# Decode attention in 2048-key steps: keys turned by VectorE in 32x32 blocks, scores in 32x64 tiles of the array

## The chip, the cores and the metric

One core of one Trainium2 chip runs the whole program in one launch. The metric is the device time in microseconds (us). The kernel before took 1918.83 us, the median of 3 runs (1914.7 to 1919.68).

## The reference, cut to what matters

The program is one inference step of a two-layer decoder: layer 0 is multi-head latent attention (MLA), layer 1 a recurrent block. It runs for a prompt of 1024 tokens and for 8 decode sequences of 8 new tokens each. Each decode sequence has 8192 past tokens, kept in pages of 128 tokens: 256 numbers of compressed latent (`ckv`) and 64 of rotated key (`kpe`) per token, all fp32. The change is in what the 8 sequences do with these pages:

```python
DEC_BATCH, DEC_SEQ, PAST_LEN, PAGE_SIZE = 8, 8, 8192, 128
N_HEADS, KV_LORA, QK_ROPE = 8, 256, 64
def attend_sample(q_lat, q_pe, ckv_past, kpe_past, ckv_new, kpe_new):
    s_past = mla_scores(q_lat, q_pe, ckv_past, kpe_past)   # q_lat.ckv + q_pe.kpe, scaled
    s_new = jnp.where(causal, mla_scores(q_lat, q_pe, ckv_new, kpe_new), NEG_INF)
    p = jax.nn.softmax(jnp.concatenate([s_past, s_new], axis=-1), axis=-1)
    return p_past @ ckv_past + p_new @ ckv_new             # the latents are keys and values
def mla_out(o_lat, z, w_uv, w_o):
    v = einsum('bthc,chv->bthv', o_lat, w_uv)
    return (v * silu(z)) @ w_o
# ckv_past = cache_ckv[page_table], kpe_past = cache_kpe[page_table]: pages in random order
```

With 8 heads and 8 tokens a sequence has 64 query rows, so two sequences (a pair) fill the 128 partitions of a score tile.

## The kernel before, in words

The program is a row of parts with a barrier between them: modulation, the input projection of layer 0, the latents, prompt attention, decode attention, the output projection of layer 0 (`out0`), and then the parts of layer 1. Inside a part each engine has its own instruction list, written in program order, and semaphores tie the lists together. So the order on an engine is the order in which the code is written.

`decode_attention` runs a hardware loop over 4 pairs of sequences. For each pair there is a step for the new tokens and 16 steps of 512 keys (`CHUNKS`). GpSimd loads raw pages by indirect DMA (`load`, L983), four chunks at a time into one of two slots. A token then lies on a partition, while a score matmul needs features on partitions. So TensorE turns the keys (`keys`, L1164): five PSUM banks per chunk, four transposes of 128x128 against the identity in each. Two of the banks belong to each sequence's `ckv`; the fifth holds the `kpe` of both, which GpSimd has put side by side before (L1003). ScalarE and VectorE copy these banks into `kT` (`keep_keys`, L1040: three on ScalarE, two on VectorE).

`scores` is then one matmul of 128x128 by 512 for `kpe` (L1179) and four of 128x64 by 512 for `ckv` (`both`, L1142), two for each sequence. `both` puts the two sequences into the left and right half of the array's columns. VectorE finds the row maximum (`maximum`, L1092 to L1096), ScalarE computes the exponential (L1061) and the factor that corrects earlier steps (L1059). TensorE turns the probabilities (`turn`, L1195), VectorE copies them out of PSUM (`keep_probs`, L1104), TensorE multiplies them by the raw pages (`values`, L1142, again through `both`), and VectorE adds the result to the running output (`accumulate`, L1114 and L1117). TensorE's order for chunk x is: `keys(x, 1..4)`, `turn(x)`, `keys(x+1, 0)`, `scores(x+1)`, `values(x)`. After the last pair a product with `w_uv` (L1232) and a multiplication by the gate (L1134) end the part.

`out0` multiplies the gated rows by `w_o`: SP loads the weights in eight pieces into three buffers (L1282), ScalarE and VectorE split each piece into a high and a low part, and TensorE runs three products for each piece. The gated prompt rows stay in the SBUF tensor `u_T` from prompt attention on.

Of the kernel before, what the change touches and what calls it, by code (L numbers as in the profile page):

```python
# [22 lines left out]
ds = bass.ds  # L23
# [475 lines left out]
def latents(nc, bank, io, k, u_T, a, outs):  # L499
# [3 lines left out]
    with ExitStack() as ctx:  # L503
# [17 lines left out]
        with nc.Block() as block:  # L521
# [18 lines left out]
            def _(act):  # L540
# [7 lines left out]
                act.activation(a["kpe_s"][:], kpe[:, NP:T], ACT.Copy).then_inc(kpe_hi, 1)  # L548
                for t in range(NT):
                    n, b = (P if t < 8 else NS), t % 2  # L550
                    act.wait_ge(rows_turned, t + 1)
                    if t >= 2:
                        act.wait_ge(rows_stored[b], 32 * (t // 2))
                    act.activation(rows_out[0:n, b, :], bank[0:n, t % 4, 0:KVL + ROPE], ACT.Copy).then_inc(rows_kept, 1)

            @block.vector
            def _(dve):
# [8 lines left out]
                dve.tensor_scalar(a["parts"][:].rearrange("p (b g s) -> p b s g", s=2, g=GROUPS),  # L566
                                  bank[:, 7, 0:NB * GROUPS].rearrange("p (b s g) -> p b s g", s=2, g=GROUPS),
                                  float(PPP), k["part_of_page"][:], ALU.mult, ALU.add).then_inc(pages_d, 1)
# [29 lines left out]
            def _(pe):  # L598
# [4 lines left out]
                pe.wait_ge(pages_d, 3)  # L603
# [26 lines left out]
def prompt_attention(nc, bank, io, k, u_T, a):  # L630
# [8 lines left out]
    with ExitStack() as ctx:  # L639
# [17 lines left out]
        unit, a_ev, d_ev, qpe_zero = sem("unit"), sem("a_ev"), sem("d_ev"), sem("qpe_zero")  # L657
        s_done, rowmax, m_done, e_done, r_done, pn_done = (sem(n) for n in ("s_done", "rowmax", "m_done", "e_done", "r_done", "pn_done"))
        pt_ps, pt_hi_d, pt_lo_d, pv_done, o_out = (sem(n) for n in ("pt_ps", "pt_hi_d", "pt_lo_d", "pv_done", "o_out"))
        A_N, D_N = 12, 16  # L660
# [5 lines left out]
        with nc.Block() as block:  # L666
            @block.sync
            def _(sp):
# [10 lines left out]
                load(0)  # L679
                with sp.Fori(1, NPAIR) as pr:  # L680
                    sp.wait_ge(unit, pr * U)
                    load(pr)

# [49 lines left out]
            def _(dve):  # L733
                dve.memset(a["qpe"][:], 0.0).then_inc(qpe_zero, 1)
                dve.wait_ge(qpe_zero, 1)
                with dve.Fori(0, NPAIR) as pr:
# [16 lines left out]
                    for h in range(2):  # L753
                        for q in range(2):

                            dve.tensor_copy(a["qpe"][ROPE * q:ROPE * q + ROPE, :, ds(pr * 2 * NTOK + (ROPE * q + NTOK * h), NTOK)],
                                            pe_rot[ROPE * h:ROPE * h + ROPE, NP:T].rearrange("p (c q t) -> p c q t", q=2, t=NTOK)[:, :, q, :]
                                            ).then_inc(d_ev, 1)
# [41 lines left out]
                    for h in range(2):  # L800
                        dve.tensor_copy(a["qlat"][:, :, :, ds(pr * 2 * NTOK + NTOK * h, NTOK)],
# [13 lines left out]
            def _(pe):  # L815
                with pe.Fori(0, NPAIR) as pr:
# [35 lines left out]
                    pe.wait_ge(d_ev, pr * D_N + 12)  # L852
                    project(1, lambda c: w_uk[:, c, P:2 * P], kv, VC, 256)
                    pe.wait_ge(d_ev, pr * D_N + 13)
# [51 lines left out]
                    pe.wait_ge(d_ev, pr * D_N + 16)  # L906
# [13 lines left out]
def decode_attention(nc, bank, io, k, u_T, a, outs):  # L920
# [7 lines left out]
    NPAIR, CHUNKS, SLOTS = NB // 2, PAGES // 4, 2  # L928
    STEPS, BLOCKS = CHUNKS + 1, 5
    S_BANK, PT_BANK, O_BANK, T_BANK = 0, 2, 3, 4  # L930
    HALF = H * NTOK
    with ExitStack() as ctx:
        sb = lambda n, shape, dt=F32: ctx.enter_context(nc.sbuf_tensor(n, shape, dt))
        sem = k["semaphore"]
        ckv = sb("ckv_pages", [P, SLOTS, 2, PAGE // PPP, KVL])
        kpe_raw = sb("kpe_pages", [P, SLOTS, 2, PAGE // PPP, ROPE])
        zero = sb("zero", [P, 2])
        kT = sb("k_T", [P, 2, BLOCKS, 512])

        free = u_T[:, 0:QC, :].rearrange("p c t -> p (c t)")  # L940
        prob = free[:, 0:1024].rearrange("p (b n) -> p b n", b=2)
        probT = free[:, 1024:2048].rearrange("p (b n) -> p b n", b=2)
        w_uv = free[:, 2048:4096].rearrange("p (c n) -> p c n", c=VC)
        kpe_r = u_T[:, N_M, 0:1024].rearrange("p (b j s e) -> p b j s e", b=2, j=4, s=2)
        o_T = u_T[:, KPE_M, 0:1024].rearrange("p (c b q) -> p c b q", c=VC, b=NB)
        parts_next = sb("parts_next", [P, 8], I32)
        tick = sb("tick", [1, 1])
        ticked, parts_set, kpe_pair_set = sem("ticked"), sem("parts_set"), sem("kpe_pair_set")
        s_new = sb("s_new", [P, NTOK])
# [866 lines left out]
```

## Time and profile before

| what | value |
|---|---|
| time, median of 3 runs | 1918.83 us (1914.7 to 1919.68) |
| span of the profiled execution | 1918.3 us |
| TensorE matmul busy, whole span | 1617.1 us (84%) |
| VectorE, ScalarE, GpSimd busy, whole span | 796.3, 627.4, 223.0 us |
| prompt attention | 347.0 to 776.4 us |
| decode attention | 776.4 to 1324.6 us |
| `out0` | 1324.6 to 1451.0 us |

The span is the time on the chip from the first to the last instruction of the profiled execution; it lies 0.5 us under the median. PE is TensorE's matmul side and PEld its weight loads, DVE is VectorE, ACT ScalarE, POOL GpSimd and SP the engine that issues most DMAs. A busy share over the whole span mixes parts with different limits, so the readings below are of the decode part. The stretch between two parts is found where all engines wait for the barrier. A record of an fp32 matmul stands for one of its two passes, so eight records are four matmuls.

### The profile page before, as it was taken

How to read it: one execution, taken by the hardware profiler on the slowest of the kernel's cores; microseconds unless marked ns; L12 is line 12 of the kernel's file. 1: busy time of each engine (PE TensorE's matmuls, PEld its weight loads, DVE VectorE, ACT ScalarE, POOL GpSimd, SP SyncE). 2: the span in 40 equal slices, each digit the busy share in tenths (PEclk: the TensorE clock that was granted, in tenths of full speed). 3: DMA queues.
4: the chain of work that ended last, by engine and by line, in shares of the span. 5: the costliest groups of instructions: out<-in, count | busy, mean ns of one | idle time of the engine just before them, and what ended most of it. 6: DMA issues, size and time to landing. Idle time of an engine off the chain costs nothing. (4 is left out here: it accounts for less than half of the span.)

```text
span 1918.3 us, 26899 instructions
## 1 busy us (share of the span) xinstructions
PE 1617.1 (84%) x10091; PEld 1274.6 (66%) x10091; DVE 796.3 (42%) x1403; ACT 627.4 (33%) x1022; POOL 223.0 (12%) x219
## 2 busy tenths in 40 slices
PE   4779996688889798599898998998996999870497
PEld 1379995577777677466555565655875999870285
DVE  1240003364645537255444454544226541239633
ACT  3231212142333324233333332333433232355232
POOL 0000000000000000222222222220121000006121
PEclk7779997799989899699999999998998999995699
DMA  9821100110100000525253245222322111100322
GB/s 333 299 56 45 44 22 24 57 28 1 27 0 27 0 0 0 243 110 220 111 201 143 115 201 217 113 110 80 118 72 64 44 44 33 44 1 0 123 88 77
DMA packets 80578, 169.42 MB, mean 88 GB/s; under 512 B 9941, under 2 KB 51803, under 8 KB 76410
## 3 DMA queue, kind: packets, MB, share of 16 engines
q1 hardware_dynamic: 71290, 84.49, 13.4%
q0 software_dynamic: 9216, 83.89, 10.9%
q8 instruction: 55, 0.90, 0.2%
q14 instruction: 17, 0.14, 0.0%
HBM read 157.91 MB, written 10.45 MB: 88 GB/s over the span
## 5 line engine op out<-in xcount | busy, mean ns | idle before, releaser
L80 PE MATMUL bank<-in_x_hi,in_w_hi 128*128 128x272 f32 x992 | 289.8, 292 | 19.9 <-DVE in_x_lo L413 19.8
L82 PE MATMUL bank<-in_x_hi,in_w_lo 128*128 128x272 f32 x992 | 288.8, 291 | 0.0
L81 PE MATMUL bank<-in_x_lo,in_w_hi 128*128 128x272 f32 x992 | 287.4, 290 | 0.0
L80 PEld LDWEIGHTS bank<-in_x_hi,in_w_hi 128*128 128x128 f32 x992 | 188.6, 190 | 20.5 <-issue 19.8
L81 PEld LDWEIGHTS bank<-in_x_lo,in_w_hi 128*128 128x128 f32 x992 | 188.9, 190 | 0.0
L82 PEld LDWEIGHTS bank<-in_x_hi,in_w_lo 128*128 128x128 f32 x992 | 188.4, 190 | 0.0
L1164 PE MATMUL bank<-c_ident,ckv_pages 128*128 128x128 f32 x1024 | 143.0, 286 | 12.4 <-DMA ckv_pages<-in_cache_ckv,page_parts 12.4
L1040 ACT ACTIVATE k_T<-bank 128x512 f32<-128x512 f32 x192 | 114.3, 598 | 109.8 <-PE bank L1164 109.8
L1164 PEld LDWEIGHTS bank<-c_ident,ckv_pages 128*128 128x128 f32 x1024 | 119.5, 147 | 35.8 <-issue 23.1
L403 DVE TENSOR_TENSOR in_w_lo<-in_w_raw,in_w_hi 128x1024 fp32r<-128x1024 f32 x31 | 37.9, 1224 | 239.2 <-ACT in_w_hi L355 239.1
L1142 PE MATMUL bank<-k_T,q_pair 128*64 128x512 f32 x512 | 124.5, 607 | 0.0
L1142 PE MATMUL bank<-ckv_pages,u_T 128*64 128x256 f32 x1024 | 121.6, 379 | 3.1 <-DVE u_T L1104 3.1
L80 PE MATMUL bank<-out_w_hi,out_g_hi 128*128 128x512 f32 (+1 forms) x288 | 114.8, 398 | 6.5 <-DVE out_w_lo L1391 6.5
L1092 DVE TENSOR_REDUCE d_stat<-bank 128x1 f32<-128x512 f32 x64 | 44.3, 691 | 178.0 <-PE bank L1142 178.0
L1142 PEld LDWEIGHTS bank<-ckv_pages,u_T 128*64 128x64 f32 x1024 | 73.4, 137 | 65.8 <-issue 34.2
L81 PE MATMUL bank<-out_w_lo,out_g_hi 128*128 128x512 f32 (+1 forms) x288 | 113.6, 394 | 0.0
L82 PE MATMUL bank<-out_w_hi,out_g_lo 128*128 128x512 f32 (+1 forms) x288 | 113.5, 394 | 0.0
L355 ACT ACTIVATE in_w_hi<-in_w_raw 128x1024 fp32r<-128x1024 f32 x31 | 32.8, 1059 | 240.2 <-PE bank L82 203.5
L1040 DVE COPY k_T<-bank 128x512 f32<-128x512 f32 x128 | 88.3, 691 | 37.1 <-PE bank L1164 31.7
L1003 POOL TENSOR_TENSOR u_T<-kpe_pages,zero 128x512 f32<-128x512 f32 x64 | 66.3, 1045 | 254.2 <-PE bank L1164 170.9
L823 PE MATMUL bank<-u_T,w_q 128*128 128x272 f32 x384 | 92.3, 401 | 3.1 <-DVE q_lo L739 3.1
L1059 ACT ACTIVATE d_stat<-d_stat 128x1 f32<-128x1 f32 x64 | 18.8, 295 | 228.6 <-DVE d_stat L1096 228.6
(272 smaller groups left out, 2950.4 us busy)
## 6 DMA issues: line engine op xcount, KB each, us to landing
u_T<-in_w_ada SPq DMA_DIRECT2D x12, 2048.0 KB, 14.3
in_w_raw<-in_r_w_in SPq DMA_DIRECT2D x16, 512.0 KB, 3.9
in_w_raw<-in_a_w_in SPq DMA_DIRECT2D x15, 512.0 KB, 4.0
x_tiles<-in_x_prompt SPq DMA_DIRECT2D x8, 512.0 KB, 9.3
out_w_raw<-in_a_w_o SPq DMA_DIRECT2D x8, 512.0 KB, 3.6
out_x_in<-in_x_prompt SPq DMA_DIRECT2D x8, 512.0 KB, 4.0
x_mid<-out_x_new SPq DMA_DIRECT2D x8, 512.0 KB, 2.9
u_T<-in_r_w_o SPq DMA_DIRECT2D x8, 512.0 KB, 8.4
```

The costliest lines, as they stand in the source:

```text
L80: pe.matmul(out, w_hi, x_hi, start=start, stop=False)
L81: pe.matmul(out, w_hi, x_lo, start=False, stop=False)
L82: return pe.matmul(out, w_lo, x_hi, start=False, stop=stop)
L355: act.activation(w_hi[:, b, :, :], w_raw[:, b, :, :], ACT.Copy).then_inc(w_hi_done, 1)
L403: dve.tensor_tensor(w_lo[:, b, :, :], w_raw[:, b, :, :], w_hi[:, b, :, :].bitcast(F32), ALU.subtract).then_inc(w_lo_done, 1)
L823: mm = pe.matmul(r[:, q, 0:cols], weights(c), x[:, c, cols * q:cols * q + cols], start=(c == 0), stop=(c == nch - 1))
L1003: pool.tensor_tensor(kpe_r[:, c % 2, :, :, :].rearrange("p j s e -> p s j e"), kpe_raw[:, c // 4 % SLOTS, :, 4 * (c % 4):4 * (c % 4) + 4, ...
L1040: ins = eng.activation(dst, src, ACT.Copy) if eng is nc.scalar else eng.tensor_copy(dst, src)
L1059: act.activation(col(CORR, x), col(M, x - 1), ACT.Exp, scale=SCALE, bias=col(NM, x)).then_inc(corr_d, 1)
L1092: dve.tensor_reduce(col(RM), bank[:, S_BANK + x % 2, :], AX.X, ALU.max).then_inc(rmax_d, 1)
L1142: mm = pe.matmul(out[HALF * s:HALF * s + HALF, :], w(s), x(s), start=start, stop=stop, tile_position=(0, HALF * s))
L1164: mm = pe.transpose(bank[:, T_BANK + n % 4, P * j:P * j + P], src, k["ident"][:])
```

## The change

Decode attention is written anew. A step now has 2048 keys of a pair of sequences, 16 steps in all, 4 for a pair, unrolled. What takes the place of what:

- Pages: GpSimd issues four indirect loads of 1 MB a step into 12 units (three steps' worth) and two of 0.5 MB for `kpe` into one buffer each.
- Keys: VectorE transposes 32x32 blocks straight from the raw pages in SBUF (`keys_T`), 10 blocks of 32 features for two sequences, 20 instructions of 128x512 a step, into a ring of 7 blocks. TensorE no longer turns keys, nothing is copied out of PSUM for them, and GpSimd's reordering of `kpe` goes.
- Since each 32-partition strip then holds other keys, the queries are copied into all four strips (`qrep`, 24 small DMAs for a pair, issued by SP). A score matmul is 32 rows by 64 columns by 512 keys; eight of them (4 strips x 2 sequences) belong to a block, and each strip writes a PSUM bank of its own (banks 0 to 3).
- The maximum and the exponential take 128x2048 in one instruction. The probabilities are turned in four groups of four, each copied out of PSUM by ScalarE.
- The new tokens' scores and values are added to the first step of a pair.
- The gated prompt rows are stored to DRAM pair by pair in prompt attention (the last store is waited for there). `out0` loads them back tile by tile on SP's queue, ahead of the weights for the first two tiles, and has six weight buffers instead of three. Two small copies (`z_s`, `k_new`) and two more index computations go into the latents.

Core of the diff (removed lines that the section on the kernel before tells of are left out):

```diff
-    NPAIR, CHUNKS, SLOTS = NB // 2, PAGES // 4, 2
-    STEPS, BLOCKS = CHUNKS + 1, 5
+    NPAIR, STEPS, PER = NB // 2, NB // 2 * GROUPS, GROUPS
+    KEYS, J, BLK, RING, UNITS = GP * PAGE // 4, PAGE // PPP, 10, 7, 12
...
+                def queries(pr):
+                    for q in range(4):
+                        rows = slice(SQ * q, SQ * q + SQ)
+                        for bb in range(4):
+                            sp.dma_start(qrep[rows, pr % 2, :, 2 * bb:2 * bb + 2, :].rearrange("p s v q -> p s (v q)"),
+                                         a["qlat"][SQ * bb:SQ * bb + SQ, 2 * pr:2 * pr + 2, :, :].rearrange("p s v q -> p s (v q)")
...
+                queries(0)
                 sp.dma_start(ckv_new[:], outs[4][0].rearrange("b t c -> t b c")).then_inc(new_in, 16)
+                queries(1)
                 sp.dma_start(w_uv, io["a_w_uv"][0].rearrange("(k p) h n -> p k (h n)", p=P)).then_inc(wuv_in, 16)
+                for pr in range(2, NPAIR):
+                    sp.wait_ge(s_blk, BLK * PER * (pr - 1))
+                    queries(pr)
...
+                def keys_T(n, blocks):
+                    for b in blocks:
+                        at = BLK * n + b
+                        if at >= RING:
+                            dve.wait_ge(s_blk, at - RING + 1)
+                        for s in range(2):
...
+                            dve.transpose(kT[:, at % RING, s, :].rearrange("p (j c) -> p j c", c=SQ), src).then_inc(t_done, 1)
...
+                keys_T(0, range(BLK))
+                for n in range(STEPS):
+                    maximum(n)
+                    if n + 1 < STEPS:
+                        keys_T(n + 1, range(4))
+                    if n:
+                        accumulate(n - 1)
+                    if n + 1 < STEPS:
+                        keys_T(n + 1, range(4, BLK))
...
+                def scores(n):
...
+                    for b in range(BLK):
+                        at = BLK * n + b
+                        pe.wait_ge(t_done, 2 * at + 2)
+                        for q in range(4):
+                            rows = slice(SQ * q, SQ * q + SQ)
+                            for s in range(2):
+                                mm = pe.matmul(bank[HALF * s:HALF * s + HALF, q, :], qrep[rows, pr % 2, s, b, :], kT[rows, at % RING, s, :],
+                                               start=b == 0, stop=b == BLK - 1, tile_position=(SQ * q, HALF * s))
+                        mm.then_inc(s_blk, 1)
...
+                scores(0)
+                for n in range(STEPS):
+                    turn(n)
+                    if n + 1 < STEPS:
+                        scores(n + 1)
+                    if n % PER == 0 and n:
+                        finish(n // PER - 1)
+                    values(n)
...
+                    sp.wait_ge(o_out, pr * 8)
+                    store(pr - 1)
+                sp.wait_ge(o_out, NPAIR * 8)
+                store(NPAIR - 1)
+                sp.wait_ge(g_out, 16 * NPAIR)
...
-        NRAW = KC if final else 3
+        NRAW = KC if final else 6
...
+                for t in range(0 if final else 2):
+                    sp.dma_start(g_raw[:, t, :, :], g_T[0].rearrange("c p t -> p c t")[:, :, t * P:t * P + P]).then_inc(g_ld[t], 16)
```

How TensorE's list changes. First one 512-key chunk of the kernel before, as written; four of these make 2048 keys (the names behind "waits" are of semaphores that several parts share; x2 or x7 behind a row counts equal rows that follow):

```order
L1164 MATMUL bank<-c_ident,ckv_pages 128x128 [waits part_out]
L1164 MATMUL bank<-c_ident,ckv_pages 128x128 x3
L1164 MATMUL bank<-c_ident,u_T 128x128 [waits x_in1]
L1164 MATMUL bank<-c_ident,u_T 128x128 x3
L1195 MATMUL bank<-c_ident,u_T 128x128 [waits ident_in,x_turned]
L1195 MATMUL bank<-c_ident,u_T 128x128 x3
L1179 MATMUL bank<-k_T,qpe_pair 128x512 [waits x_turned,sq_done]
L1142 MATMUL bank<-k_T,q_pair 64x512 x4
L1142 MATMUL bank<-ckv_pages,u_T 64x256 [waits d_o_done,ident_in]
L1142 MATMUL bank<-ckv_pages,u_T 64x256 x7
```

Then TensorE in one 2048-key step of the changed kernel: turning the probabilities of step n (L1169), the scores of step n+1 (L1159, here two of the ten blocks), the values of step n (L1189, here the first two of four groups):

```order
L1169 MATMUL bank<-c_ident,u_T 128x128 [waits d_pt_sb,gate_b_in]
L1169 MATMUL bank<-c_ident,u_T 128x128 x3
L1169 MATMUL bank<-c_ident,u_T 128x128 [waits d_pt_sb]
L1169 MATMUL bank<-c_ident,u_T 128x128 x3
L1159 MATMUL bank<-u_T 64x512 [waits xn_done,gate_b_in]
L1159 MATMUL bank<-u_T 64x512 x7
L1159 MATMUL bank<-u_T 64x512 [waits xn_done]
L1159 MATMUL bank<-u_T 64x512 x7
L1189 MATMUL bank<-ckv_pages,u_T 64x256 [waits d_pt_sb,d_o_done]
L1189 MATMUL bank<-ckv_pages,u_T 64x256 x7
L1189 MATMUL bank<-ckv_pages,u_T 64x256 [waits d_pt_sb]
L1189 MATMUL bank<-ckv_pages,u_T 64x256 x7
```

The twenty key transposes and the `kpe` matmul of each chunk are gone from TensorE; each block of eight score matmuls now waits for VectorE's transposes (`t_done`, shown as xn_done).

VectorE in a chunk of the kernel before, with the two key copies (L1040), the probabilities' copy, the maximum and the accumulation:

```order
L1040 COPY k_T<-bank 128x512 [waits ms_done,part_done]
L1040 COPY k_T<-bank 128x512 [waits part_done]
L1104 COPY u_T<-bank 128x512 [waits gate_b_in,x_out]
L1092 TENSOR_REDUCE d_stat<-bank 128x1 [waits ms_done]
L1094 TENSOR_TENSOR d_stat<-d_stat 128x1 [waits rstd_done]
L1096 TENSOR_SCALAR d_stat<-d_stat 128x1 [waits modt_done]
L1114 SCALAR_TENSOR_TENSOR d_stat<-d_stat 128x1 [waits mod_kept,x_turned]
L1117 SCALAR_TENSOR_TENSOR o_acc<-o_acc,d_stat,bank 128x256 [waits d_o_done,gate_b_in]
```

VectorE in a step of the changed kernel: the maximum of step n over 2048 keys (L1083 to L1087), then the transposes of step n+1, of which the first eight stand before the accumulation of step n-1 and twelve behind it (the last two pairs of these are of `kpe`):

```order
L1083 TENSOR_REDUCE d_stat<-bank 128x1 [waits x_turned]
L1084 TENSOR_TENSOR d_stat<-d_stat 128x1 [waits d_own]
L1087 TENSOR_SCALAR d_stat<-d_stat 128x1 [waits d_own]
L1071 STREAM_TRANSPOSE u_T<-ckv_pages 128x512 [waits w_ada_in3,w_ada_in2,x_turned]
L1071 STREAM_TRANSPOSE u_T<-ckv_pages 128x512 [waits x_in1,x_in0]
L1071 STREAM_TRANSPOSE u_T<-ckv_pages 128x512 [waits x_turned]
L1071 STREAM_TRANSPOSE u_T<-ckv_pages 128x512
L1098 TENSOR_TENSOR d_stat<-d_stat 128x1 [waits modt_done,gate_b_in]
L1100 COPY o_acc<-bank 128x256 [waits d_pv_h]
L1071 STREAM_TRANSPOSE u_T<-kpe_pages 128x512 [waits part_done,x_turned]
L1071 STREAM_TRANSPOSE u_T<-kpe_pages 128x512 [waits part_out]
```

VectorE's three copies a chunk give way to 20 transposes a step; x_turned is here `s_blk`, the count of scored blocks, which frees a place in the ring of seven.

## Rows read from the trace of the kernel before

**Rows 1.** Windows: stretch, us, busy us PE PEld DVE ACT POOL, clock, DMA, GB/s.
```profile
776.40:1324.60 548.20, 504.32 (x3300) 309.96 (x3300) 247.32 (x557) 181.13 (x408) 131.09 (x151) 0.95 0.39 156
784.00:788.00 4.00, 0.00 (x0) 0.00 (x0) 0.00 (x0) 0.00 (x0) 2.64 (x3) 0.50 1.02 426
56.30:59.40 3.10, 3.09 (x17) 0.60 (x16) 0.00 (x0) 2.17 (x3) 0.00 (x0) 0.61 1.05 388
```
**Rows 2.** Waits in the decode part: total us, times, longest us.
```profile
ACT d_stat L1059 <- DVE d_stat L1096: 228.6, 64, 5.0
DVE d_stat L1092 <- PE bank L1142: 178.0, 64, 4.8
PE bank L1164 <- DMA ckv_pages<-in_cache_ckv,page_parts: 12.4, 1, 12.4
```
**Rows 3.** Timeline of TensorE over one 512-key chunk: start us, us, instructions.
```profile
808.35 1.90 PE L1142 MATMUL bank<-ckv_pages,u_T 128*64 128x256 f32 x16
810.18 1.53 PE L1164 MATMUL bank<-c_ident,ckv_pages 128*128 128x128 f32 x12
811.55 0.60 PE L1164 MATMUL bank<-c_ident,u_T 128*128 128x128 f32 x4
811.98 0.60 PE L1195 MATMUL bank<-c_ident,u_T 128*128 128x128 f32 x4
812.42 0.60 PE L1164 MATMUL bank<-c_ident,ckv_pages 128*128 128x128 f32 x4
813.02 1.10 PE L1179 MATMUL bank<-k_T,qpe_pair 128*128 128x512 f32 x2
814.04 1.94 PE L1142 MATMUL bank<-k_T,q_pair 128*64 128x512 f32 x8
815.81 1.90 PE L1142 MATMUL bank<-ckv_pages,u_T 128*64 128x256 f32 x16
```
**Rows 4.** Timeline of TensorE in the modulation: eight matmuls in 32-column tiles.
```profile
56.30 3.09 PE L253 MATMUL bank<-u_T,c_T 128*32 128x512 f32 x16
```
**Rows 5.** Groups of VectorE by line and shape: busy us, mean ns, idle before.
```profile
L1092 DVE TENSOR_REDUCE d_stat<-bank 128x1 f32<-128x512 f32 x64 | 44.3, 691 | 178.0 <-PE bank L1142 178.0
L769 DVE TENSOR_REDUCE att_stat<-bank 128x1 f32<-128x1024 f32 x8 | 9.8, 1224 | 1.1
L779 DVE TENSOR_SCALAR prob<-prob,att_stat 128x512 f32<-128x512 f32 x8 | 3.9, 486 | 0.3
L1639 DVE TENSOR_TENSOR_SCAN lru_r<-lru_a,u_T 128x1024 f32<-128x1024 f32 x8 | 24.4, 3044 | 0.0
L1094 DVE TENSOR_TENSOR d_stat<-d_stat 128x1 f32<-128x1 f32 x64 | 10.6, 166 | 2.2
L1117 DVE SCALAR_TENSOR_TENSOR o_acc<-o_acc,d_stat,bank 128x256 f32<-128x256 f32 x64 | 30.7, 480 | 37.8 <-PE bank L1142 37.8
```
**Rows 6.** Groups of ScalarE by line and shape.
```profile
L711 ACT ACTIVATE prob<-bank,att_stat 128x1024 f32<-128x1024 f32 x8 | 8.9, 1114 | 0.0
L711 ACT ACTIVATE prob<-bank,att_stat 128x128 f32<-128x128 f32 x8 | 3.0, 370 | 6.7 <-DVE att_stat L772 6.7
L1040 ACT ACTIVATE k_T<-bank 128x512 f32<-128x512 f32 x192 | 114.3, 598 | 109.8 <-PE bank L1164 109.8
```
**Rows 7.** Timeline at the start of the decode part.
```profile
777.26 1.12 POOL L983 DMA_INDIRECT ckv_pages<-in_cache_ckv,page_parts  x1 [0.72 <-POOL zero L975]
793.79 3.68 PE L1164 MATMUL bank<-c_ident,ckv_pages 128*128 128x128 f32 x16 [12.38 <-DMA ckv_pages<-in_cache_ckv,page_parts]
```
**Rows 8.** Timeline at its end: last values, then the product with w_uv.
```profile
1312.95 1.95 PE L1142 MATMUL bank<-ckv_pages,u_T 128*64 128x256 f32 x16 [0.78 <-DVE u_T L1104]
1317.05 5.99 PE L1232 MATMUL bank<-u_T 128*128 128x64 f32 x32 [0.67 <-ACT u_T L1072]
```
**Rows 9.** DMA issues: KB each, us from issue to landing.
```profile
x_mid<-out_x_new SPq DMA_DIRECT2D x8, 512.0 KB, 2.9
```
**Rows 10.** Costliest groups: the first product of an output projection.
```profile
L80 PE MATMUL bank<-out_w_hi,out_g_hi 128*128 128x512 f32 (+1 forms) x288 | 114.8, 398 | 6.5 <-DVE out_w_lo L1391 6.5
```
**Rows 11.** Costliest groups: weight loads of the values product.
```profile
L1142 PEld LDWEIGHTS bank<-ckv_pages,u_T 128*64 128x64 f32 x1024 | 73.4, 137 | 65.8 <-issue 34.2
```

More of the change, by code:

```diff
@@ new lines, in _ @@
+                own = Chain(dve, own_d)
+                def keys_T(n, blocks):
[4 more added lines that the diff above has]
+                        for s in range(2):
+                            if b == 0:
+                                for half in range(2):
+                                    dve.wait_ge(ckv_in[unit(n, s, half)], 16 * (n // 3 + 1))
+                            if b == 8:
+                                dve.wait_ge(kpe_in[s], 16 * (n + 1))
+                            if b < 8:
+                                u, c0 = unit(n, s, 0), P * (b % 2) + SQ * (b // 2)
+                                src = ckv[:, u:u + 2, :, c0:c0 + SQ].rearrange("p u j c -> p (u j) c")
+                            else:
+                                src = kpe[:, s, :, SQ * (b - 8):SQ * (b - 8) + SQ]
+                            dve.transpose(kT[:, at % RING, s, :].rearrange("p (j c) -> p j c", c=SQ), src).then_inc(t_done, 1)
@@ new lines, in new_scores @@
+                        seq, out = 2 * pr + s, bank[HALF * s:HALF * s + HALF, X_BANK, 0:NTOK]
+                        new = slice(NTOK * seq, NTOK * seq + NTOK)
+                        pe.matmul(out, a["qpe"][:, seq, :], a["kpe_s"][0:ROPE, new], start=True, stop=False, tile_position=(0, HALF * s))
+                        for v in range(VC):
+                            mm = pe.matmul(out, a["qlat"][:, seq, v, :], a["k_new"][:, v, new], start=False, stop=v == VC - 1,
+                                           tile_position=(0, HALF * s))
@@ new lines, in values @@
+                def values(n):
+                    pr, g = divmod(n, PER)
+                    if n:
+                        pe.wait_ge(o_done, n)
+                    halves = [slice(HALF * s, HALF * s + HALF) for s in range(2)]
+                    if g == 0:
+                        pe.wait_ge(ptn_sb, pr + 1)
+                        for s in range(2):
+                            pe.matmul(bank[halves[s], O_BANK, 0:KVL], p_new_T[:, halves[s]], ckv_new[:, 2 * pr + s, :], start=True, stop=False,
+                                      tile_position=(0, HALF * s))
+                    for j in range(J):
+                        if j % 4 == 0:
+                            pe.wait_ge(pt_sb, 4 * n + j // 4 + 1)
+                        for s in range(2):
+                            mm = pe.matmul(bank[halves[s], O_BANK, 0:KVL], probT[:, P * j + HALF * s:P * j + HALF * s + HALF],
+                                           ckv[:, unit(n, s, j // 8), j % 8, :], start=g > 0 and j == 0, stop=j == J - 1,
+                                           tile_position=(0, HALF * s))
+                        if j % 8 == 7:
+                            mm.then_inc(pv_h, 1)
@@ L1228, in _ @@
+                finish(NPAIR - 1)
                 pe.wait_ge(wuv_in, 16)
@@ L1705, in build, with rows_of @@
         x_mid = nc.dram_tensor("x_mid", [T, D], F32).ap()
+        gated = nc.dram_tensor("gated", [KC, P, NP], F32).ap()
+        def rows_of(prompt, decode):
+            return lambda t: decode if isinstance(t, int) and t == NT - 1 else prompt[ds(t * P, P), :]
         with ExitStack() as mla:
```

478 lines of the change are left out of this document (202 added, 276 removed).

## The prediction, made before the changed kernel ran

> **What bounds the kernel now.** I read the windows first: decode takes 548.2 us, and TensorE has matmuls in flight for 504.3 of them, while VectorE is busy 247.3 and ScalarE 181.1 [rows 1]. The waits say the same from the other side: VectorE's maximum waits 178.0 us for TensorE's scores, ScalarE 228.6 us for VectorE, but TensorE itself has only one large wait, 12.4 us for the first pages [rows 2]. So TensorE's own list is the length of this part. One chunk of that list, from one `values` to the next, takes 815.81 - 808.35 = 7.46 us [rows 3]; 64 of them make 477 of the 548. DMA isn't near the bound: the part moves 156 GB/s on average and 426 in a loaded stretch [rows 1]. A 2048-key step needs 5.24 MB, which is 12.3 us at that rate.
>
> **Where a chunk goes.** From start to start of the groups [rows 3]: `values` 1.83, sixteen `ckv` transposes and four of `kpe` 1.37 + 0.43 + 0.60 = 2.40, turning the probabilities 0.44, the `kpe` matmul 1.02, the four `ckv` score matmuls 1.77. Four chunks are 29.84 us.
>
> **TensorE's new step.** The transposes of keys and the `kpe` matmul go. `values` is unchanged: 4 x 1.83 = 7.32. Turning needs 16 transposes, 4 x 0.44 = 1.76; but the third group waits for ScalarE's first copy out of PSUM and the fourth for the second, at 0.60 each [rows 6], so I take 2.5. The scores are the doubtful term. Ten blocks of eight matmuls of 32 rows by 64 columns replace the rest. In the trace two matmuls that lie side by side in the columns cost as much as one: four of them in 1.77 us is 0.88 a pair, no more than the full-width `kpe` matmul's 1.02 [rows 3]. And eight matmuls in 32-column tiles took 3.09 us at a granted clock of 0.61 [rows 1, 4]; one after another at even full speed they would take 8 x 0.88 = 7.0. So column tiles run at once, four of them too. Tiles that differ in rows are not in the trace. If the four strips also run at once, a block is one pair's time, 0.88, and I take 0.90 for the starts of eight tiles; if the strips queue behind one another it is 4 x 0.88 = 3.5. I take 0.90: the nearest row, the four column tiles, shows the array running as many tiles as it is cut into. Scores are then 9.0, and with 0.3 for the changes of tile shape a step is 9.0 + 2.5 + 7.3 + 0.3 = 19.1 us in place of 29.84.
>
> The Trainium skill, "TensorE: Matmul & The Clock Gate", Part 3 (Measured speedup vs the span model), lists four row tiles of 32 rows with 512 columns at 3.07 times the speed of one, not 4. By that page a block would be 0.88 x 4 / 3.07 = 1.15, an estimate, and the time about 1756 us. No run before shows four row tiles.
>
> **VectorE's new step.** Its new work is 20 transposes of 128x512 from SBUF to SBUF. No row shows one. The cheapest row of that size is 0.486 (a multiplication by a scalar, SBUF to SBUF); the dearest per element is the scan, 3.044 for 1024, so 1.52 for 512 [rows 5]. The nearest rows are plain reads of 512 elements, at 0.69. I take 0.70: 14.0 us. The maximum over 2048 continues 0.691 at 512 and 1.224 at 1024 by 1024 x 1.04 ns to 2.29. Three small instructions at about 0.17 (as L1094) and the accumulation's 0.48 add 1.0, so 17.3 us of work. After the last transpose VectorE waits until that block is scored, some 1.3, before the next maximum: 18.6. That is just under TensorE's 19.1, so the two engines nearly tie, and each 0.01 us on a transpose above about 0.725 adds 0.2 to every step.
>
> **ScalarE's chain.** Between the last block of step n+1 and turning it stand the maximum chain, 2.3 + 0.35, and the exponential over 2048. That one continues 0.370 at 128 and 1.114 at 1024, 0.83 ns for an element, to 1.96 [rows 6]; with the read of its sum some 2.2. Together 5.0, and `values(n)` at 7.3 lies beside it. If that cover went, it would be 5.0 a step. GpSimd's reordering disappears, but nothing waited for it on the path.
>
> **The decode part, from its start.** The first pages came 793.79 - 776.40 = 17.4 us into the part before, after two `ckv` loads and two of `kpe` [rows 7]; the first three of the new loads, each half as large, let VectorE begin, and I take +15. SP has 24 small copies of queries to issue first, before the new tokens' latents; I take them as covered by these 15 us. Twenty transposes, 14.0, and the last block: the first scores end at +30. The maximum and twenty transposes more: the second end at +47.7. Fourteen steps at 19.1 are 267.4, so +315.1. Then values 7.3, turn 2.5, values 7.3 and the tail. From the end of the last `values` (1312.95 + 1.95) to the end of the part it took 9.7 before [rows 1, 8], and that work is unchanged: +341.9. Three further pair starts at about 1.3 (new tokens' scores, two transposes of the output) make 346. That is 202 us less than 548.2.
>
> **The rest.** The stores of gated rows overlap the next pair, but the last is waited for: 2.9 for 512 KB [rows 9] and 1.2 for as much again at 426 GB/s, +4.1. Two copies of 128x512 in the latents: 2 x 0.60 [rows 6] = +1.2. In `out0` the six weight buffers can take back at most the 6.5 us that both output projections wait for split weights [rows 10], and two 512 KB tiles ahead of the weights delay the first by 2.5 at 426 GB/s, up to 5 with their short runs. I take -2, with -6.5 and +5 as ends. Prompt attention loses two small VectorE copies a pair, which I count as nothing, since VectorE waits there. Sum: -202 + 4.1 + 1.2 - 2 = -199. From the span of 1918.3 that gives 1719.6, and with the 0.5 by which the median lies over the span, 1720 us.
>
> **Rivals.**
> 1. *The strips queue.* Nothing in the trace excludes it. A block is then 3.5 and a step 35 + 10.1 = 45; the first scores end at +50, the second 7.5 + 35 later, fourteen steps add 631 and the end 31: about 755 against 548, so near 2128 us, slower. With a block at b the part is about 195 + 160b, which passes 548 at b = 2.2: from there the kernel is slower. 6 in 100.
> 2. *The strips overlap in part.* If two of the sixteen weight loads of a block, 0.137 each [rows 11], aren't hidden, it is 0.90 + 0.27 = 1.17; 2.7 more a step, 15 times, less what VectorE's near tie takes up anyway, is some 38: 1758 us. That loads of weights run under matmuls in flight (the part has 310.0 us of them and still 504.3 of matmuls in 548.2 [rows 1]) speaks against it, the number of small instructions in a block for it. The page of the skill named above lands near the same time by its own figure. 14 in 100.
> 3. *VectorE becomes the bound.* At t for a transpose its step is 20t + 4.6. With 0.85 it is 21.6, 2.5 more than 19.1, and with the dearer first two steps some 42: 1762 us. With 1.0 it is 24.6, 1810 us. At the scan's 1.52 it is 35, and the whole comes to about 1980, slower; the turn lies near 1.35. 17 in 100, of which 2 beyond the turn. The Trainium skill, "VectorE: DVE Perf Modes" (The three transpose paths), gives 311 ns for a 128x128 transpose of 2-byte numbers; four of them would be 1.24, an estimate, and the time about 1885. "Vector Engine (DVE) Microarchitecture Reference", § 3.8, says instead that the transpose sustains one element per cycle and lane, by which it is no dearer than a copy. The plain reads at 0.69 are what the rows have.
> 4. *The queries come late.* If the 24 small copies land behind the 12 MB of pages, which take 30 us at 426 GB/s, the first scores end at +40 instead of +30: 1730 us. 10 in 100.
>
> **How the numbers follow.** The forecast has 53 in 100, with its own range 1698 to 1740: down to 1698 if transposes cost 0.6, blocks 0.86 and turning 2.0, up to 1740 with a step of 19.8 and the dear end of `out0`. Rivals 2 and 4 and the cheap half of 3 lie below 1800, so the range is 1692 to 1800, which leaves out rival 1, the dear half of rival 3, and little below. A difference under 0.3%, 5.8 us, can't be told from none. Slower: rival 1 and the end of rival 3, 0.08; the same, 0.02 at the turn between them; faster, 0.90.
>
> **What would show it.** A score block (L1159) of 0.9 us from the first of its eight matmuls to the next block's first; transposes (L1071) of 0.7; TensorE busy for nearly all of the decode part and VectorE over 85% of it, with short waits on either side; a step of about 19 us from one maximum to the next. The forecast is wrong if blocks take 2 us or more, if VectorE is busy throughout while TensorE waits for `t_done`, or if the decode part is far from 346 us while blocks and transposes cost what I say.

## The result, and the profile after

| | before | after |
|---|---|---|
| time, median | 1918.34 us (1914.7 to 1919.68, 4 runs) | 1727.55 us (1725.26 to 1729.77, 4 runs) |
| ratio | 1 | 0.9002, 95% interval 0.8986 to 0.9017 |
| span of the profiled execution | 1918.3 us | 1728.0 us |
| latents, from first to last instruction (as in the rows below) | 47.0 us | 47.7 us |
| prompt attention | 427.8 us | 429.5 us |
| decode attention | 547.6 us | 350.3 us |
| `out0` | 125.9 us | 125.6 us |

The kernel is 10% faster; 1720 us was forecast. The modulation, in which nothing changed, took 102.5 us in the profile of before and 107.2 in that of after. Over all kernels profiled here it varies between 102.5 and 107.2, so 4.7 us of the comparison of spans is not owed to the change.

Two windows of the changed kernel, with the columns of [rows 1]: the decode part (351 us here, with the barrier at its end) and its steady middle. The clock is the granted clock of TensorE as a share of 2.4 GHz: 0.50 is the 1.2 GHz level.

```profile
783.30:1134.30 351.00, 304.98 (x3948) 165.99 (x3949) 244.93 (x417) 73.24 (x124) 90.07 (x96) 0.94 0.71 251
857.00:1100.00 243.00, 239.25 (x3170) 128.92 (x3169) 195.91 (x335) 58.14 (x99) 69.31 (x75) 1.00 0.78 282
```

In that middle VectorE's maximum still waits for TensorE's scores (columns of [rows 2]):

```profile
DVE d_stat L1083 <- PE bank L1159: 44.1, 13, 3.8
```

In the middle TensorE is busy 239 of 243 us at the full clock. It is still the bound; VectorE is busy 81%. About 46 us of the part's 351 are without a matmul, most of them at the start.

One step in that middle, TensorE's timeline; [rows 3] is the answering piece of before:

```profile
999.71 5.57 PE L1189 MATMUL bank<-ckv_pages,u_T 128*64 128x256 f32 x50
1005.21 1.09 PE L1169 MATMUL bank<-c_ident,u_T 128*128 128x128 f32 x8
1006.61 1.14 PE L1169 MATMUL bank<-c_ident,u_T 128*128 128x128 f32 x8 [0.31 <-ACT u_T L1042]
1007.69 8.84 PE L1159 MATMUL bank<-u_T 32*64 32x512 f32 x160
1016.46 7.13 PE L1189 MATMUL bank<-ckv_pages,u_T 128*64 128x256 f32 x64
1023.51 1.09 PE L1169 MATMUL bank<-c_ident,u_T 128*128 128x128 f32 x8
```

Turning takes 1007.69 - 1005.21 = 2.48 us, the ten blocks of scores 1016.46 - 1007.69 = 8.77, so 0.877 a block, and the values 1023.51 - 1016.46 = 7.05. The 0.31 is the wait for ScalarE's copies out of PSUM.

The groups that answer to [rows 5, 6]:

```profile
L1071 DVE STREAM_TRANSPOSE u_T<-ckv_pages 128x512 f32<-128x512 f32 x256 | 155.6, 675 | 33.8 <-DMA ckv_pages<-in_cache_ckv,page_parts 20.5
L1159 PE MATMUL bank<-u_T 32*64 32x512 f32 x2560 | 144.4, 600 | 0.0
L1028 ACT ACTIVATE u_T<-bank,d_stat 128x2048 f32<-128x2048 f32 x16 | 31.5, 1968 | 201.1 <-DVE d_stat L1087 201.1
```

The record of a transpose lasts 0.675 us on average; back to back the records overlap, and 256 of them keep VectorE busy for 155.6 us, 0.61 each. The end of the part, to be read beside [rows 8]:

```profile
1119.66 7.13 PE L1189 MATMUL bank<-ckv_pages,u_T 128*64 128x256 f32 x64
1128.83 3.76 PE L1218 MATMUL bank<-u_T 128*128 128x64 f32 x32 [0.56 <-ACT u_T L1047]
```

And the largest wait that TensorE has in the decode part, with the columns of [rows 2]:

```profile
PE bank L1137 <- DMA ckv_new<-out: 38.6, 1, 38.6
```

It began 5.5 us before the part, so 33.1 of it lie in the part, where the pages' 12.4 us stood before: the first scores wait for the new tokens' latents, 64 KB. The start in the timeline of VectorE, SP and TensorE:

```profile
796.83 0.71 DVE L1071 STREAM_TRANSPOSE u_T<-ckv_pages 128x512 f32<-128x512 f32 x1 [18.48 <-DMA ckv_pages<-in_cache_ckv,page_parts]
799.15 0.49 SPq L987 DMA_DIRECT2D ckv_new<-out  x1
799.61 7.83 DVE L1071 STREAM_TRANSPOSE u_T<-ckv_pages 128x512 f32<-128x512 f32 x13 [2.06 <-DMA ckv_pages<-in_cache_ckv,page_parts]
816.41 0.38 PE L1137 MATMUL bank<-kpe_new,qpe_T 64*64 64x8 f32 x2 [38.63 <-DMA ckv_new<-out]
818.07 11.80 PE L1159 MATMUL bank<-u_T 32*64 32x512 f32 x160
820.19 1.30 DVE L1071 STREAM_TRANSPOSE u_T<-ckv_pages 128x512 f32<-128x512 f32 x2 [12.76 <-PE bank L1159]
830.00 2.29 DVE L1083 TENSOR_REDUCE d_stat<-bank 128x1 f32<-128x2048 f32 x1 [4.84 <-PE bank L1159]
```

Below, +13 means 13 us after the start of the part.

The pages are there at 796.83, 13.5 us into the part, and VectorE fills its ring of seven blocks (14 transposes) by 807.4. Then it waits 12.76 us, because no block is scored. `ckv_new` is issued at 799.15, behind 24 copies of queries, and lands 17 us later. The first scores end at 829.9, 46.6 us into the part.

What shares the DMA engines with the copies is in the next rows: GpSimd's next loads of pages, and the packets of the pages (q0, from GpSimd) and of the copies (q1, from SP), with their MB and share of the 16 engines' time, first from 800 to 810, then from 812 to 816:

```profile
824.58 0.94 POOL L1010 DMA_INDIRECT kpe_pages<-in_cache_kpe,page_parts  x1 [28.17 <-DVE u_T L1071]
```

```profile
q0 software_dynamic: 571, 3.69, 96.1%
q1 hardware_dynamic: 571, 0.18, 8.1%
```

```profile
q1 hardware_dynamic: 1531, 0.57, 99.9%
q0 software_dynamic: 47, 0.25, 17.5%
```

GpSimd stands for 28.17 us before the third load of `kpe`, until VectorE has read the first. So ten loads are ahead of the copies, 9.4 MB and not the 12 of the fourth rival. While they stream, the two queues move the same number of packets, but a packet of pages has 6.5 KB on average and one of the copies 0.3 KB: the copies get 5% of the bytes. When the pages end, the copies' packets go nearly seven times as fast, 383 a us instead of 57. That is in line with copies that land only with the last pages; the second experiment tests it.

### The profile page after: what moved, and what is told of

Read it like the earlier page. It is cut to its first block and busy times, and to the rows that moved or that the text cites. A ratio compares the mean times of both kernels' runs of the same rounds, so it can differ in the third digit from the quotient of the medians.

```text
span 1728.0 us, 26291 instructions
## 1 busy us (share of the span) xinstructions
PE 1413.8 (82%) x10739; PEld 1128.7 (65%) x10739; DVE 793.1 (46%) x1256; ACT 520.4 (30%) x740; POOL 181.9 (11%) x164
## 3 DMA queue, kind: packets, MB, share of 16 engines
q1 hardware_dynamic: 88378, 95.50, 17.3%
## 5 line engine op out<-in xcount | busy, mean ns | idle before, releaser
L1071 DVE STREAM_TRANSPOSE u_T<-ckv_pages 128x512 f32<-128x512 f32 x256 | 155.6, 675 | 33.8 <-DMA ckv_pages<-in_cache_ckv,page_parts 20.5
L1159 PE MATMUL bank<-u_T 32*64 32x512 f32 x2560 | 144.4, 600 | 0.0
L1003 POOL DMA_INDIRECT ckv_pages<-in_cache_ckv,page_parts x64 | 60.1, 939 | 770.3 <-POOLq L1699 670.5
L1189 PE MATMUL bank<-ckv_pages,u_T 128*64 128x256 f32 x1024 | 114.0, 381 | 0.0
L1159 PEld LDWEIGHTS bank<-u_T 32*64 32x64 f32 x2560 | 55.6, 134 | 77.0 <-issue 61.9
L1189 PEld LDWEIGHTS bank<-ckv_pages,u_T 128*64 128x64 f32 x1024 | 72.1, 137 | 45.3 <-issue 10.6
L1028 ACT ACTIVATE u_T<-bank,d_stat 128x2048 f32<-128x2048 f32 x16 | 31.5, 1968 | 201.1 <-DVE d_stat L1087 201.1
L831 PEld LDWEIGHTS bank<-u_T,w_q 128*128 128x128 f32 x384 | 74.2, 195 | 19.9 <-DVE q_lo L750 4.8
L735 ACT ACTIVATE pt_hi<-bank 128x512 fp32r<-128x512 f32 (+2 forms) x96 | 43.8, 489 | 119.9 <-PE bank L889 119.9
L1321 POOL TENSOR_TENSOR out_x_new<-out_x_new,out_x_in 128x1024 f32<-128x1024 f32 (+1 forms) x18 | 43.0, 2386 | 245.9 <-DVE out_x_new L1408 245.9
```

The costliest lines, as they stand in the source:

```text
L735: act.activation(pt_hi[:, 4 * g:4 * g + n, slot:slot + P], bank[:, 4 + gi % 2, 0:P * n].rearrange("p (j q) -> p j q", q=P), ACT.Copy).then ...
L831: mm = pe.matmul(r[:, q, 0:cols], weights(c), x[:, c, cols * q:cols * q + cols], start=(c == 0), stop=(c == nch - 1))
L1003: pool.indirect_dma_start(ckv[:, u, :, :].rearrange("p j c -> p (j c)"), None, io["cache_ckv"][0].rearrange("n (q j) c -> (n q) (j c)", q= ...
L1071: dve.transpose(kT[:, at % RING, s, :].rearrange("p (j c) -> p j c", c=SQ), src).then_inc(t_done, 1)
L1159: mm = pe.matmul(bank[HALF * s:HALF * s + HALF, q, :], qrep[rows, pr % 2, s, b, :], kT[rows, at % RING, s, :], start=b == 0, stop=b == BLK ...
L1189: mm = pe.matmul(bank[halves[s], O_BANK, 0:KVL], probT[:, P * j + HALF * s:P * j + HALF * s + HALF], ckv[:, unit(n, s, j // 8), j % 8, :], ...
```

## The experiments

**Is it the latents alone that are late?** TensorE's wait for them is moved to where the values product needs them.

```diff
-                pe.wait_ge(new_in, 16)
                 scores(0)
...
+                        if pr == 0:
+                            pe.wait_ge(new_in, 16)
                         pe.wait_ge(ptn_sb, pr + 1)
```

> The changed kernel, but TensorE waits for the new tokens' latents (ckv_new) only where their values product needs them, not ahead of the first scores. In the changed kernel that wait was 38.6 us. Theory (all small copies of SP lie behind the 12 MB of pages): the 24 copies of queries land no earlier than ckv_new does, so TensorE now waits for them instead; the first scores start at most 3 us earlier and the time stays within 1723 to 1731 us. Rival (ckv_new alone is late, because it is issued 25th): the queries are there by about +22 us in the decode part, the first scores start some 9 us earlier, and the time is near 1718 us.

1729.14 us, one run. The wait only changed its name:

```profile
811.74 11.07 PE L1159 MATMUL bank<-u_T 32*64 32x512 f32 x160 [31.29 <-DMA u_T<-qpe_T]
```

Its decode part begins at 778.7, so the first scores start at +33, where they started at +34.8. The queries are as late as the latents; the theory stands, with ten loads in place of its 12 MB.

**Do the small copies wait behind the pages?** On top of that edit, GpSimd holds back the pages from step 1 on (those of step 2 were behind the 28 us of standing anyway), so 5.2 MB instead of 9.4 are ahead of the copies.

```diff
                 for n in range(STEPS):
+                    if n == 1:
+                        pool.wait_ge(qrep_in[0], 16 * 24)
+                        pool.wait_ge(new_in, 16)
```

> As the run before, and GpSimd issues the pages of steps 1 and 2 only when the queries of the first pair and ckv_new have landed. Theory (small copies wait behind the pages): only 5 MB of pages are ahead of them, they land near +22 us instead of +33, the first scores end near +32 instead of +46.5, and the pages of step 1 come in time or a few us late; the time falls by 8 to 14 us, to 1714 to 1720. Rival (the copies are slow by themselves, 24 at about 0.65 us of issue and their own latency): they land at +33 as before, and the pages of step 1 come late on top, so the time rises by 5 us or more.

1717.62 us, ratio to before 0.895 (0.8935 to 0.8965), an interval that lies under that of the changed kernel. Its decode part begins at 779.1:

```profile
802.27 10.74 PE L1162 MATMUL bank<-u_T 32*64 32x512 f32 x160 [21.45 <-DMA u_T<-qpe_T]
819.27 9.01 DVE L1074 STREAM_TRANSPOSE u_T<-ckv_pages 128x512 f32<-128x512 f32 x15 [2.32 <-DMA ckv_pages<-in_cache_ckv,page_parts]
```

The queries are complete at +23, ten us sooner than with ten loads ahead of them. Of these 23 us SP's issuing takes 15.8: it issues the 24 copies from 783.33 to 799.1 in the changed kernel, and as long here. The pages of step 1 come 2.3 us late, which was the price expected.

**What if the queries are copied in good time?** The copies of pairs 0 and 1 are moved into prompt attention, right after its last pair has produced the queries. The last store moves into the decode part, and the wait for the latents moves as in the first experiment (the last not in the diff).

```diff
-                sp.wait_ge(o_out, NPAIR * 8)
-                store(NPAIR - 1)
-                sp.wait_ge(g_out, 16 * NPAIR)
+                sp.wait_ge(g_out, 16 * (NPAIR - 1))
+                sp.wait_ge(d_ev, NPAIR * D_N)
+                for pr in range(2):
+                    copy_queries(sp, u_T, a, pr, q_out)
+                sp.wait_ge(q_out, 16 * 48)
...
-                queries(0)
                 sp.dma_start(ckv_new[:], outs[4][0].rearrange("b t c -> t b c")).then_inc(new_in, 16)
-                queries(1)
+                sp.dma_start(a["gated"].rearrange("c p t -> p c t")[:, KC - 2:KC, :], u_T[:, N_M - 2:N_M, 0:NP]).then_inc(st_out, 16)
+                sp.wait_ge(st_out, 16)
```

> The queries of pairs 0 and 1 are copied in prompt attention, as soon as its last pair has produced them (they have 100 us of cover there); the last store is issued in the decode part, behind ckv_new; and ckv_new is waited for only by the first values product. Theory (the late queries cost all of what the first scores lost, and nothing else is late there): the first scores follow VectorE's transposes and end about 30 us into the decode part instead of 46.5, decode takes some 335 us, prompt attention 4 us less, the time is 1704 to 1711. Rival (the next thing is late: the pages of steps 1 and 2 beside the 1 MB store, or TensorE at the low clock): the first two scores end later than +32 and +50, and the time is 1712 to 1720.

1710.84 us (1706.79 to 1720.07 over 5 runs), ratio to before 0.8924 (0.8902 to 0.8946). This is faster than the kernel before and the changed kernel. Its profile is of the fastest of the five runs and that of the changed kernel of the slowest of four, so the parts are compared and not the spans. The decode part takes 336.0 us, 14.3 less than in the changed kernel, and prompt attention 422.2:

```profile
792.99 11.79 PE L1165 MATMUL bank<-u_T 32*64 32x512 f32 x160 [17.94 <-DVE u_T L1076]
804.88 2.29 DVE L1088 TENSOR_REDUCE d_stat<-bank 128x1 f32<-128x2048 f32 x1 [1.03 <-PE bank L1165]
```

The part begins at 773.5. The two other edits by themselves left the decode part at 350.0 (the store, next run) and 352.0 (the latents' wait, first run), so the 14 us need the copies moved; what that brings with the latents' wait in its old place wasn't run. TensorE now waits for VectorE's transposes, and the first scores end at +31.3, where the prediction had put them (+30).

**The last store by itself.** As in the run just told, without moving the queries.

> The changed kernel, but the last store of gated rows (1 MB) is issued in the decode part, behind the queries, and is no longer waited for at the end of prompt attention. Theory (that wait is the 4.1 us of the prediction, and nothing in decode needs the store before its fifth step): prompt attention ends about 4 us earlier, the decode part stays at 349 to 352 us, the time is 1722 to 1725. Rival (the 1 MB only adds to the traffic in which the queries are already late): decode grows by as much, and the time stays within 1726 to 1731.

1723.9 us, ratio 0.8983 (0.8966 to 0.9001), an interval that overlaps that of the changed kernel, so the parts have to decide. Prompt attention took 422.0 us, decode 350.0. In the changed kernel the last instruction of VectorE in prompt attention ends at 778.34 and the next part begins at 783.3; before, these were 775.40 and 776.4 [rows 1]. The wait thus costs about 4, as the theory has it. The rest of the 7.5 us by which this profile's prompt attention is shorter isn't explained: in the other kernels, which keep the store's wait, it varied from 426.6 to 432.6, and the run with the queries in prompt attention, which has no such wait either, took 422.2.

**Do the strips run at once?** Strips 2 and 3 are left out after the first block.

```diff
-                        for q in range(4):
+                        for q in range(2 if b else 4):
```

> Leaves out half of the scores: strips 2 and 3 are scored in the first of the ten blocks only, so nine blocks have four matmuls instead of eight. Theory (the strips run at once, a block lasts as long as one pair of column tiles): a block stays at 0.88 us, the step at 18.3 us and the time at 1722 to 1730 us. Rival (the strips share the array's time): a block falls to about 0.45 us, the scores to about 5 us, and the step to VectorE's pace of about 16.7, so the time falls by 20 us or more, below 1708.

1737.04 us, one run: with half the matmuls the scores take as long as before, 871.77 - 863.02 = 8.75 us against 8.77:

```profile
818.08 17.34 PE L1159 MATMUL bank<-u_T 32*64 32x512 f32 x88
863.02 8.81 PE L1159 MATMUL bank<-u_T 32*64 32x512 f32 x88
871.77 7.13 PE L1189 MATMUL bank<-ckv_pages,u_T 128*64 128x256 f32 x64
```

So a block lasts as long with two strips as with four, and as long as one pair of column tiles (0.88 [rows 3]). The time missed the expected 1722 to 1730, and the first row says where: the first scores took 17.34 us instead of 11.80, at a low clock. Windows of this run from the first score matmul on and of the third scores:

```profile
818.00:824.00 6.00, 6.00 (x38) 1.87 (x41) 3.06 (x5) 0.00 (x0) 0.00 (x0) 0.50 0.45 122
824.00:830.00 6.00, 6.00 (x32) 1.72 (x28) 1.06 (x4) 0.00 (x0) 4.25 (x5) 0.50 0.73 254
830.00:836.00 6.00, 5.43 (x28) 1.23 (x20) 0.50 (x1) 0.00 (x0) 1.35 (x2) 0.50 0.99 391
863.00:871.70 8.70, 8.70 (x89) 2.97 (x88) 5.22 (x9) 0.73 (x2) 1.94 (x3) 1.00 0.98 382
```

And of the changed kernel:

```profile
818.00:824.00 6.00, 6.00 (x58) 2.01 (x65) 3.01 (x5) 0.00 (x0) 0.00 (x0) 0.50 0.44 110
824.00:830.00 6.00, 5.87 (x112) 1.87 (x96) 1.12 (x5) 0.00 (x0) 4.20 (x5) 0.99 0.81 261
```

With two strips the granted clock stays at 0.50, the 1.2 GHz level, all through the first scores; with four it was 0.99 from the seventh us on. In both runs TensorE had stood for 38 us before, but for 1.7 us of the new tokens' scores. The third scores ran at 1.00 with two strips too, so two strips don't hold the clock down once it is up.

**What would strips in turn cost?** Each strip's matmuls wait for those of the strip before.

```diff
                         for q in range(4):
+                            if q:
+                                pe.wait_ge(strip, 3 * at + q)
...
-                        mm.then_inc(s_blk, 1)
+                            mm.then_inc(strip if q < 3 else s_blk, 1)
```

> Each strip's two matmuls of a block wait until those of the strip before have ended, so the four strips run in turn; the result is the same. This prices the prediction's first rival. Theory (the strips' concurrency is worth 3 x 0.88 us a block, and a wait for one's own result costs something on top): a block takes 3.5 to 4.2 us, 160 of them add 420 to 530 us, the time is 2145 to 2260 us, slower than the kernel before. Rival (the strips shared more of the array's time than the trace shows, and running alone each is shorter): a block of 2.5 or less, under 1990 us.

2591.58 us, one run, far above what was expected. A stretch of scores and the windows say why:

```profile
899.38 46.37 PE L1162 MATMUL bank<-u_T 32*64 32x512 f32 x118
```

```profile
900.00:950.00 50.00, 48.11 (x136) 7.64 (x134) 3.22 (x5) 0.00 (x0) 1.87 (x2) 0.50 0.07 21
1500.00:1550.00 50.00, 48.23 (x190) 13.16 (x182) 11.47 (x19) 4.79 (x8) 3.75 (x4) 0.60 0.17 60
```

118 records are 7.4 blocks, so a block takes 6.3 us. The price was worked out at the full clock, 4 x 0.88, but TensorE ran at a granted clock of 0.50 to 0.60, though matmuls were in flight 48 of 50 us. At 0.50 a pair takes 1.73 (the 17.34 us above, for ten blocks), so four in turn would take 6.9: the low clock accounts for the excess over 3.5. So the run shows that strips held in turn by waits make the kernel slower than the one before, but not what they would cost at the full clock, and why the clock stays low isn't shown.

**How far is VectorE from being the bound?** Three runs: four transposes of a step done twice, eight done twice, and eight cut to 32 of 512 elements (the last not in the diff). Each was run once.

```diff
+                            if n and 4 <= b < 6:      # the second run: b < 8
+                                own.step(dve.transpose(kT[:, at % RING, s, :].rearrange("p (j c) -> p j c", c=SQ), src))
                             dve.transpose(kT[:, at % RING, s, :].rearrange("p (j c) -> p j c", c=SQ), src).then_inc(t_done, 1)
```

> Four transposes of a step (blocks 4 and 5) are done twice, 24 instead of 20; the result is the same. A transpose measured 0.605 us from start to start, and one that is waited for 0.67. Theory (VectorE's step is its work plus about 1.3 us of waiting for the last block, 20 x 0.605 + 4.6 = 16.7, beside TensorE's 18.3): it becomes 16.7 + 4 x 0.67 = 19.4, 1.1 over TensorE, so 15 steps add about 16 us: 1740 to 1748 us. Rival (all of the 3.2 to 3.7 us that VectorE waits at each maximum is free): 2.7 us fit in, and the time stays within 1723 to 1731.

> Eight transposes of a step are done twice, 28 in all; the result is the same. Theory (VectorE's step is 16.7 + 8 x 0.67 = 22.1, 3.8 above TensorE's): 15 steps add 57 us, the time is 1775 to 1792 us, and the rise over the run with four more (1745.5) is about 40. Rival (more of VectorE's waiting is free, and four more cost what they did for another reason): under 1765.

> From step 1 on, 8 of the 20 transposes of a step turn 32 of their 512 elements only, so their blocks are scored with stale keys; this takes about 4 us from VectorE's step of 16.7. Theory (TensorE's list is the bound, with VectorE 1.6 us a step behind it): the step stays at 18.3 us and the time at 1722 to 1731 us. Rival (the two engines nearly tie, as the prediction put it, and each waits for the other in turn): the step falls by 0.5 us or more and the time below 1720.

Four more: 1745.49 us, a step in the middle of a pair 964.13 - 944.74 = 19.39 from one maximum to the next (19.4 expected):

```profile
944.74 2.29 DVE L1085 TENSOR_REDUCE d_stat<-bank 128x1 f32<-128x2048 f32 x1 [1.28 <-PE bank L1161]
964.13 2.29 DVE L1085 TENSOR_REDUCE d_stat<-bank 128x1 f32<-128x2048 f32 x1 [1.27 <-PE bank L1161]
```

Eight more: 1794.17 us, slightly over the range; steps of 22.4 to 23.9 where 22.1 was expected, and 48.7 us over the run with four more where about 40 was. So the formula is 0.3 to 1.8 us a step short there. TensorE now waits twice in the scores for a block:

```profile
860.75 5.41 PE L1161 MATMUL bank<-u_T 32*64 32x512 f32 x96
866.93 1.12 PE L1161 MATMUL bank<-u_T 32*64 32x512 f32 x16 [0.77 <-DVE u_T L1073]
869.61 3.49 PE L1161 MATMUL bank<-u_T 32*64 32x512 f32 x48 [1.56 <-DVE u_T L1073]
```

Eight shorter: 1730.77 us, the step 883.62 - 865.31 = 18.31, as in the changed kernel:

```profile
865.31 2.29 DVE L1084 TENSOR_REDUCE d_stat<-bank 128x1 f32<-128x2048 f32 x1 [4.38 <-PE bank L1160]
883.62 2.29 DVE L1084 TENSOR_REDUCE d_stat<-bank 128x1 f32<-128x2048 f32 x1 [4.38 <-PE bank L1160]
```

So TensorE bounds the step with VectorE about 1.6 us behind; that holds for the 20 transposes as they are.

**Six or three weight buffers in `out0`.**

```diff
-        NRAW = KC if final else 6
+        NRAW = KC if final else 3
```

> The changed kernel with three weight buffers in out0, as before, instead of six. The prediction took the six buffers for up to 6.5 us. Theory (splitting the weights on ScalarE and VectorE, 1.06 and 1.22 us a piece, sets the pace, not their loads): out0 stays within 2 us of 125.5, the time within 1726 to 1731. Rival (loads set the pace, and the six buffers gave back what the tiles ahead of them cost): out0 grows by 4 to 6 us, the time to 1731 to 1734.

1733.24 us, ratio 0.9024 (0.9007 to 0.904). `out0` took 129.0 us against 125.6: between the two, nearer to the rival. The waits of TensorE in `out0`, before the edit (the changed kernel) and after it:

```profile
PE bank L80 <- DVE out_w_lo L1396: 4.5, 1, 4.5
```

```profile
PE bank L80 <- DVE out_w_lo L1396: 6.0, 4, 4.0
```

With six buffers only the first product waits. The waits make 1.5 of the 3.4 us. The rest is in the matmuls, as the windows of the part show, changed kernel first:

```profile
1134.30:1259.90 125.60, 114.15 (x512) 88.22 (x512) 33.72 (x44) 50.70 (x65) 21.49 (x9) 0.95 0.43 138
```

```profile
1135.50:1264.50 129.00, 116.17 (x512) 88.68 (x512) 34.08 (x44) 51.02 (x65) 21.47 (x9) 0.94 0.42 135
```

They are busy 2.0 us longer with three buffers, at a granted clock of 0.73 in the first 10.7 us against 0.84; whether the buffers cause that isn't shown. The run doesn't settle the comparison of times, since its interval overlaps that of the changed kernel; the part's length is the finer measure.

## Why the prediction was right

Its mechanism holds: the strips run at once, and TensorE's shorter list is the bound. That the number is as near is partly luck, since two errors offset each other: the start of the decode part cost 16 us more than forecast, the steps and the end about 11 less. By its steps:

- *TensorE's new step.* The doubtful term was the block, taken as 0.90; it is 0.877. Turning 2.5, measured 2.48; values 7.32, measured 7.05. The step of 19.1 is 18.3 in the middle of a pair. With the pair starts the 14 steps took 847.2 to 1110.3, 263.1 us, against 14 x 19.1 + 3.9 = 271. The experiment with half the strips shows that the four strips run at once: the first two rivals are out. The Trainium skill's figure for four row tiles, 3.07 ("TensorE: Matmul & The Clock Gate", Part 3), which would make a block 1.15, an estimate, doesn't show in this stream of blocks at 0.877.
- *VectorE's new step.* A transpose was taken as 0.70 from the reads of 512 elements. A record lasts 0.675, and back to back they start every 0.60 (13 in 7.83). So the work is some 15.4 us and not 17.3, and the near tie was none: cutting eight transposes changed nothing, and adding four gave the 16.7 + 4 x 0.67 = 19.4 that the formula has with the measured durations. The Trainium skill's 311 ns for a 128x128 transpose of 2-byte numbers ("VectorE: DVE Perf Modes", The three transpose paths), scaled by size, would give 1.24, an estimate; 0.675 was measured. ScalarE's chain is 4.85 by its own terms and not 5.0; TensorE stood 4.95 for it after the first scores, and no term of the sum uses it.
- *The start.* This is the step that failed: "I take them as covered by these 15 us". Issuing the 24 copies alone takes SP 15.8 us. The first pages came at +13.5 (+15 forecast), but the queries and latents at +33, and the first scores ended at +46.6 instead of +30. Rival 4 had this mechanism, with a price of 10 us and 10 in 100. Its 12 MB are 9.4, and they moved at 387 GB/s beside the copies (3.69 and 0.18 MB in 10 us) and not at 426; it put the copies at +30 and ten blocks at 10 us, where +33.1, 1.7 for the new tokens' scores and 11.8 for ten blocks, the first four at the low clock, make the +46.6. So it costs 16.6 at the first scores, and moving the copies took the first scores to +31.3 and 14.3 us off the part. So rival 4 came true inside a forecast whose other terms nearly held.
- *The end of the part.* 26.8 us were taken from the last scores on; 1110.2 to 1134.3 is 24.1. The product with `w_uv` took 3.76 us instead of 5.99, at a granted clock of 1.00 where it was 0.60 before.
- *The signs.* Blocks, transposes and steps came out as it said. VectorE was to be busy for over 85% of the part and is for 70%, 81% in the middle; TensorE, "nearly all" of it, for 87%.
- *The rest.* A store of 1 MB lands after 4.1 us, as worked out. The latents grew by 0.7 (1.2 forecast). `out0` stayed within 0.3 us (-2 forecast): its first product starts 10.3 us into the part instead of 6.1, behind the two tiles, and with six buffers the part is 3.4 shorter than with three, of which waits explain 1.5.

The span came out 8.4 us over the sum of 1719.6: 5 in decode (351 for 346), 4.7 in the unchanged modulation, 1.7 in `out0`, less 2.4 in prompt attention and 0.5 in the latents.

## What to carry to other kernels

When matmuls have a short contraction, count the tiles that the array can run at once: a block of eight 32x64 tiles cost what one pair of 128x64 tiles cost, so moving the transposes to another engine paid although each score block then covered a quarter of the features. Before starting a large transfer, list the small copies that the first instruction needs; issued beside 9.4 MB of pages, packet for packet, they arrived when the pages were done. Whether fewer and larger packets would land sooner wasn't run. And when two engines look tied, measure the slack with a run that adds work to one of them.

## What the runs showed that was not expected

- 64 KB of latents took 17 us from issue to arrival and 24 copies of 16 to 32 KB were complete only at +33 us, while the pages streamed; with 5.2 MB of pages ahead instead of 9.4 they were complete at +23. The two queues moved 571 packets each in 10 us, however small the copies' packets were.
- TensorE's clock stayed at its 1.2 GHz level in stretches where matmuls were in flight without a pause but only part of the array's rows worked: 0.50 over 18 us with two of four strips, 0.50 to 0.60 over whole steps with one strip at a time. Yet two strips ran at 1.00 later in the same run, so the cause stays open.
